# Steady FFN feature pairs: high-half and low-half products alternate step by step instead of standing in two runs

## The reference

```python
def swiglu(x, w_gate, w_up, w_down):
    return (jax.nn.silu(x @ w_gate) * (x @ w_up)) @ w_down
```

## Time and profile before

| | |
|---|---|
| median of 3 runs | 1740.89 us |
| lowest and highest run | 1740.61, 1741.8 us |
| span of the profiled execution | 1739.6 us |
| what lies around the span (median less span) | 1.3 us |
| TensorE matmul busy | 1728.8 us, 99% |
| VectorE, ScalarE busy | 1262.9 us (73%), 1003.7 us (58%) |
| high products, L1834 | x2094, 501.1 us |
| low products, L1839 | x2112, 276.8 us |

### The profile page before, as it was taken

One profiled execution on the slowest core, in us unless ns is written; L12 is line 12 of the kernel. 1 busy time (PEld: TensorE's weight loads), 2 busy tenths in 40 slices (PEclk: granted clock), 3 DMA queues, 4 the chain that ended last, 5 costly groups with the idle time before them and its releaser, 6 DMA issues.

```text
span 1739.6 us, 24239 instructions
## 1 busy us (share of the span) xinstructions
PE 1728.8 (99%) x9535; PEld 1500.2 (86%) x9535; DVE 1262.9 (73%) x1602; ACT 1003.7 (58%) x1247; POOL 58.9 (3%) x95
## 2 busy tenths in 40 slices
PE   9999999999999999999999999999999999999998
PEld 8888998888888888888889888888888988888887
DVE  6766777766677666876667898867666898876665
ACT  7544566654467444754457866464446966565444
POOL 7200000000000000000001000000000000000000
PEclk9999999999999999999999999999999999999999
DMA  7755435665545655465545544356555554446552
GB/s 244 255 189 188 162 122 170 217 222 189 191 169 181 212 187 176 144 208 185 189 145 194 184 165 145 122 186 220 190 192 170 163 176 134 138 165 215 188 186 88
DMA packets 211564, 311.65 MB, mean 179 GB/s; under 512 B 6434, under 2 KB 166112, under 8 KB 211360
## 3 DMA queue, kind: packets, MB, share of 16 engines
q1 hardware_dynamic: 207472, 303.84, 53.4%
q0 software_dynamic: 3712, 6.44, 1.2%
q10 hardware_dynamic: 304, 0.33, 0.1%
HBM read 309.54 MB, written 1.05 MB: 179 GB/s over the span
## 4 chain that ended last, share of the span: by engine, by line
PE 91%; ACT 4%; DVE 3%; issue 1%; DMA 0%; SPq 0%; DVEq 0%; ACTq 0%
PE psD L1945 28%; PE psA L1834 27%; PE psA L1839 14%; PE psA L1912 3%; PE psA L1927 3%; PE psA L1778 3%; PE psA L1945 2%; PE psD L2231 2%; PE psA L1931 1%; PE psA L1916 1%; PE psA L1783 1%; PE psA L2015 1%; ACT hi L455 1%; PE psD L2168 1%; PE psD L2015 1%
## 5 line engine op out<-in xcount | busy, mean ns | idle before, releaser
L927 DVE TENSOR_TENSOR lo<-raw,hi 128x2048 fp32r<-128x2048 f32 x285 | 650.5, 2290 | 171.9 <-ACT hi L455 171.2
L455 ACT ACTIVATE hi<-raw 128x2048 fp32r<-128x2048 f32 x285 | 542.4, 1909 | 77.2 <-PE psD L1945 33.5
L1834 PE MATMUL psA<-xT,hi 128*128 128x512 f32 x2094 | 501.1, 390 | 0.1
L1834 PEld LDWEIGHTS psA<-xT,hi 128*128 128x128 f32 x2094 | 387.2, 188 | 77.0 <-DVE xT L960 0.3
L1839 PEld LDWEIGHTS psA<-xT,lo 128*128 128x128 f32 x2112 | 271.9, 191 | 11.8 <-issue 0.5
L1839 PE MATMUL psA<-xT,lo 128*128 128x256 f32 x2112 | 276.8, 283 | 0.1
L1945 PE MATMUL psD<-hi,prod_hi 128*128 128x512 f32 x544 | 213.4, 392 | 0.0
L1945 PE MATMUL psD<-hi,prod_lo 128*128 128x512 f32 x544 | 212.6, 391 | 0.0
L1945 PE MATMUL psD<-lo,prod_hi 128*128 128x512 f32 x544 | 143.6, 389 | 0.0
L593 ACT ACTIVATE scr<-psA 128x512 f32<-128x512 f32 x66 | 39.3, 595 | 163.3 <-PE psA L1839 163.3
L608 ACT ACTIVATE prod_hi<-scr 128x512 fp32r<-128x512 f32 x66 | 41.7, 632 | 157.8 <-DVE scr L1309 157.8
(11 more groups left out here) (308 smaller groups left out, 1926.2 us busy)
## 6 DMA issues: line engine op xcount, KB each, us to landing
raw<-in_w_in SPq DMA_DIRECT2D x48, 1024.0 KB, 5.2
raw<-in_ffn_w_up SPq DMA_DIRECT2D x43, 1024.0 KB, 5.4
raw<-in_ffn_w_gate SPq DMA_DIRECT2D x43, 1024.0 KB, 5.4
raw<-in_ffn_w_down SPq DMA_DIRECT2D x43, 1024.0 KB, 5.0
raw<-in_w_gate SPq DMA_DIRECT2D x22, 1024.0 KB, 5.3
raw<-in_w_up SPq DMA_DIRECT2D x22, 1024.0 KB, 5.3
raw<-in_w_down SPq DMA_DIRECT2D x22, 1024.0 KB, 4.9
raw<-in_lru_w_in SPq DMA_DIRECT2D x10, 1024.0 KB, 5.3
```

The lines of the kernel that those rows point to most:

```text
L455: act.activation(hi[:, n % RING, :], raw_of(n), ACT.Copy).then_inc(hi_ready, 1)
L927: dve.tensor_tensor(lo[:, n % RING, :], raw_of(n), hi[:, n % RING, :].bitcast(F32), ALU.subtract).then_inc(lo_ready, 1)
L1834: pe.matmul(psA[:, bank + f, :], w_hi[:, k, f * P:(f + 1) * P], xT[:, k].rearrange("p e s -> p (e s)"), start=(k == 0), stop=False)
```

## The change

In steady blocks the 16 high and 16 low products alternate: for each group f and step k one high product, then the low product of the same f and k. The wait at the start of the block is for `lo_ready`; the wait for `hi_ready` is gone, since `lo` is made from `hi`. The `between` step of the first FFN comes after 8 high and 8 low products instead of after 8 high ones. The number, size and operands of the products are the same, and `block_used` is raised by the same last product. The hand-written first blocks, `contract` and all other functions stay.

```diff
                 else:
-                    pe.wait_ge(hi_ready, n_at)
-                    high(0, 0, KT)
-                    if between:
-                        between()
-                    high(1, 0, KT)
                     pe.wait_ge(lo_ready, n_at)
-                    low(0, 0, KT)
-                    last = low(1, 0, KT)
+                    for f in range(2):
+                        for k in range(KT):
+                            high(f, k, k + 1)
+                            last = low(f, k, k + 1)
+                        if f == 0 and between:
+                            between()
                 last.then_inc(block_used, 1)
```

## The result

The kernel after takes 1778.62 us (median of five runs, 1775.16 to 1781.51) against 1741.25 us (five runs, 1740.61 to 1741.8): ratio 1.021, 95% interval 1.0199 to 1.0221. It is 37.4 us slower. I had forecast 1760.5 us, with a range up to 1774. So the direction was right, and the size was off by nearly half: 18 of the 37 us were not in my sum.

The account below looks back on a forecast made before the run. It took TensorE, busy 1728.8 of 1739.6 us, as the bound. 1739.6 + 0 (order) + 19.4 (stalls) + 0.6 (restarts) = 1759.6 us, plus 1.3 around the span, rounded to 1760.5; range 1748 to 1774.

Parts of the forecast that it names:

- TensorE bounds, and what the order adds goes through: Whole kernel: TensorE busy 1728.8 of 1739.6 us, so added time lengthens the kernel unless it falls into 10.8 us idle.
- The wait moves to the block's start, stalls of 19.4 + 0.6 us: Up 0 and gate 2 of each FFN: TensorE waits for late lo, 19.4 us, plus 0.6 us for restarting.
- The allowance of 0.6 us: Twelve restarts of TensorE after a wait: 0 to 0.1 us each, 0.6 us together.
- I take 0 ... The two cancel as estimates: 2016 alternating pairs: 5 ns lost by the high product, about 6 ns won by the low one, so order costs 0.
- a fifth of the tail: Tail: 20 to 25 ns per return from low to high, spread over five high products; alternation pays one fifth, 5 ns.
- bounds (-23.8 and +38 us): Order of 2016 pairs: from low products' fixed part hidden, 23.8 us less, to 1890 more returns at 20 ns, 38 more.
- rival 1: Alternating blocks keep the tail of each return: 9.5 us at 5 ns, 1770, or 1798 at 20 ns; chance 0.15.
- The clock as a rival of its own: After long stalls in the first three FFNs TensorE's clock falls to 1.2 GHz: 3 to 8 us, 1766; chance 0.06.
- Rivals 2, 3 and 5: Low product cheaper, 12 us less (0.07); its fixed part hidden, -23.8 us (0.05); stalls don't come, 1741 to 1750 us (0.05).
- Rival 3: The 2016 low products' whole fixed part hides behind their neighbours: -23.8 us, which with +20 gives 1737; chance 0.05.
- the fixed 11.8 ns: Part of each TensorE product's spacing independent of its columns, worked out from 227 and 119.4 ns: 11.8 ns.
- the 1.3 us around the span: Added to the forecast span of 1759.6 us for time outside it: 1760.9, then rounded to 1760.5 us.

Follow-up runs that it names:

- e9: e1 plus filler products keeping TensorE busy ahead of the waits of gate 2 and up 0, first six loop blocks written out: 1762.81 us, ratio 1.0127.
- e10: The whole change plus the filler products and written-out blocks of e9: 1774.41 us, ratio 1.019 against the kernel before.
- e1: Kernel before with its old order of products, only the wait at a steady block's start moved to lo: 1767.17 us, ratio 1.0143.
- e6: Kernel before with 108 of 126 steady blocks in runs of two high and two low products, without the stalls: 1743.95 us, ratio 1.0016.
- e7: Kernel before with 108 of 126 steady blocks in runs of four high and four low products, without the stalls: 1749.53 us, ratio 1.0047.
- e5: Kernel before with 108 steady blocks alternating, without the stalls, their low products widened to 512 columns like the high ones: 1924.42 us, one run.
- e4: Kernel before with 108 steady blocks alternating, without the stalls, each low product from the other feature group (another bank): 1752.07 us, ratio 1.0066.

## Why the prediction was right and wrong

- *TensorE bounds, and what the order adds goes through*: right. The stalls (e9, 20.7 us), the order (e10 over e9, 11.6) and the clock (e1 over e9, 5.1) add up to 37.4 us, as measured.
- *The wait moves to the block's start, stalls of 19.4 + 0.6 us*: right in place and size. From the FFN's first block to the start of gate 2 the trace of after is late by 4.4, 3.4, 4.4 and three times 2.8 us more than before, of which about 0.3 us each are the alternation of the three blocks in between; forecast 4.25, 3.53, 4.2 and three times 2.47. e9 gives 20.7. The allowance of 0.6 us for twelve restarts had no row behind it and was half of what the traces have, 1.3 us.
- *The order, "I take 0 ... The two cancel as estimates"*: this step failed. It is 7 ns a pair, 12 to 14 us. I had the high product behind a low one at a fifth of the tail, 5 ns, and let the low one win 6. The runs showed 236.7 ns for the high product, 10 more than its 227, and 116.7 for the low one, 3 less. What I took for one tail played from its beginning each time is a pattern of three pairs in which only one low product of three has the short spacing, and each high product is long. The forecast's own bounds (-23.8 and +38 us) held it, and its rival 1 had 9.5 us for the lower form at 0.15. The mistake was to fill a gap in the rows with a cancellation of two estimates: the rows had a return after runs of four and more only, and e6 and e7 show that single products can't be inferred from them, nor from each other.
- *The clock as a rival of its own at 0.06*: this step failed too; the sum has nothing for it. It isn't an alternative to the stalls; it comes on top of them. Once I held stalls of 2 to 3 us for likely, falls of the clock belonged in the sum with their own chance. Its price was about right: 5 us in e1, where 3 to 8 stood; but stalls of 2.2 us were enough too, not just the longest ones, and the longest ones didn't always bring it. The Trainium skill, page "TensorE: Matmul & The Clock Gate", Part 1, says that the gate's window runs free of the program; that of two equal stalls in e1, at 763 and 1198 us, only the first had a fall behind it agrees with it.
- *Rivals 2, 3 and 5*: fell. The low product won 3 ns on average, the high one lost more, and no stall was absorbed. Rival 3's argument against itself is circular: the fixed 11.8 ns were worked out from the two spacings together, so they are the same for both sizes by construction.
- *The ends of the sum*: the 1.3 us around the span were a median less the span of one other execution. In every run the time is 1.75 to 1.94 us above its own span, and "rounded" took off another 0.4. That is 1 us of the miss.

The range ended at 1774 since it took its rivals one at a time; the two that came true add up to 17 us over the forecast.

What stays open is why a return costs what it does: the size of neighbours decides it (e5), the bank (e4, with the rows of after and before beside it) and the tile of the weights (e5) don't; but no run here shows what inside TensorE makes 8, 3 and 19 ns out of runs of one, two and four. Nor does a run show what decides whether the clock falls behind a given stall.

## What to carry to other kernels

When a wait for a later product of another engine moves to the front of a block, compare in the trace when that product was ready with when the block starts, for the first blocks behind each stage and not for the settled loop, and put a possible fall of the clock beside every stall of some 2 us. Don't alternate products of different size on TensorE without a trace: keep them in few long runs, and price an order that the rows don't show by a run, not by cancelling two estimates. If TensorE must wait, fillers in a free bank can pay for themselves, as in e9.

## What the runs showed of the hardware

- Products of equal size in fp32r, each with its own load of weights, stand 226.7 ns apart with 512 columns and 120 with 256; with 512 columns it makes no difference whether the weights come from one tile or from two in turn (e5). Changing between the sizes costs 19 to 20 ns per return from small to large in runs of four or more, 8 in single alternation and 3 in runs of two.
- Behind a stall the first product of 512 columns takes 335 to 338 ns until the next start, 0.11 us more than in the stream (after).
- A stall of 2.2 us between dense stretches was enough for the granted clock to fall to 1.2 GHz, in some cases and not in others; each fall cost about 1.7 us. With fillers that leave at most 1.3 us idle, all eight runs of e9 and e10 had a mean granted clock of 0.999 or more, where the nine of e1 and of the change had 0.994 to 0.998.
